# Heads of a latent attention started six turns apart instead of in pairs

## The reference

```python
def mla_attention(q, c_kv, k_rope, pos, kv_norm_w, w_uk, w_uv, q_norm_w, k_norm_w):
    ...
    ckv = rms_norm(c_kv, kv_norm_w)
    k_nope = (ckv @ w_uk).reshape(B, S, MLA_HEADS, MLA_NOPE)
    v = (ckv @ w_uv).reshape(B, S, MLA_HEADS, MLA_DV)
    k = jnp.concatenate([k_nope, jnp.broadcast_to(k_rope[:, :, None, :], (B, S, MLA_HEADS, MLA_ROPE))], axis=-1)
    q = rms_norm(q, q_norm_w)
    k = rms_norm(k, k_norm_w)
    ...
    for s0 in range(0, S, Q_BLOCK):
        s1 = s0 + Q_BLOCK
        kb, vb = k[:, :s1], v[:, :s1]
        sc = jnp.einsum('bqhd,bkhd->bhqk', q[:, s0:s1], kb, preferred_element_type=jnp.float32) * scale
        mask = chunk_id[s0:s1, None] >= chunk_id[None, :s1]
        sc = jnp.where(mask, sc, -jnp.inf)
        p = jax.nn.softmax(sc, axis=-1).astype(v.dtype)
        outs.append(jnp.einsum('bhqk,bkhd->bqhd', p, vb))
```

```python
        o_a = rms_norm(o_a, dn_norm_w[l]) * jax.nn.silu(dn_z.reshape(B, S, DN_HEADS, DN_DV))
        y_a = o_a.reshape(B, S, DN_V) @ w_out_dn[l]
        ...
        y_b = o_b.reshape(B, S, MLA_VD) @ w_out_mla[l]
        mix = jax.nn.sigmoid(gate_dn) * y_a + jax.nn.sigmoid(gate_mla) * y_b
```

## Time and profile before

| | us |
|---|---|
| median of 3 runs | 2572.59 |
| lowest and highest run | 2569.84, 2576.09 |
| profiled execution | 2570.07 |
| its span in the profile | 2568.3 |

### The profile page before, as it was taken

The page is one execution under the profiler, slowest core; times in us unless marked ns, Lnnn a source line. Parts: engine busy times, 40 slices in busy tenths (PEclk is TensorE's granted clock), DMA queues, the critical chain, the costliest instruction groups (busy, mean ns, idle before and its releaser), DMA issues.

```text
span 2568.3 us, 27012 instructions
## 1 busy us (share of the span) xinstructions
PE 2358.6 (92%) x10928; PEld 1890.4 (74%) x10928; DVE 1083.0 (42%) x1579; ACT 927.7 (36%) x1352; POOL 700.4 (27%) x417
## 2 busy tenths in 40 slices
PE   8798989997789899899999887999999999999996
PEld 4577877993467677688888676787777777888875
DVE  2476655444433432433321499513444243322333
ACT  2534424114433432533322332334552433322334
POOL 1141144001101125322223232321232353432332
PEclk9898989998899899999999898999999999999998
DMA  8222223221122123333333421232211322333341
GB/s 261 74 66 74 68 57 99 66 78 37 37 52 62 52 84 109 102 100 98 94 98 97 123 79 57 88 98 82 82 58 58 115 82 82 107 90 99 99 123 50
DMA packets 347984, 220.67 MB, mean 86 GB/s; under 512 B 18393, under 2 KB 327244, under 8 KB 347860
## 3 DMA queue, kind: packets, MB, share of 16 engines
q1 hardware_dynamic: 338462, 202.31, 27.2%
q10 hardware_dynamic: 9398, 16.62, 2.0%
HBM read 210.49 MB, written 8.41 MB: 85 GB/s over the span
## 4 chain that ended last, share of the span: by engine, by line
PE 75%; DVE 11%; ACT 8%; POOL 3%; issue 3%; DMA 1%; ACTq 0%; SPq 0%; DVEq 0%; POOLq 0%
PE ps L342 74%; DVE arena L368 4%; ACT arena L357 4%; DVE arena L360 2%; DVE scr L368 1%; PE ps L345 1%; ACT scr L357 1%; POOL wlo L360 1%; ACT whi L357 1%; ACT L353 1%; POOL arena L360 1%; DVE arena L365 1%; DVE scr L360 1%; DVE wlo L360 1%; DMA wraw<-in_w_in_dram 1%
## 5 line engine op out<-in xcount | busy, mean ns | idle before, releaser
L342 PE MATMUL ps<-hhi,whi 128*128 128x512 f32 x1664 | 679.1, 408 | 53.2 <-POOL wlo L360 30.3
L360 POOL TENSOR_TENSOR wlo<-wraw,whi 128x1024 fp32r<-128x1024 f32 (+1 forms) x164 | 391.2, 2385 | 1188.7 <-ACT whi L357 1188.7
L342 PE MATMUL ps<-hlo,whi 128*128 128x512 f32 x1664 | 662.8, 398 | 0.0
L342 PE MATMUL ps<-hhi,wlo 128*128 128x512 f32 x1664 | 661.7, 398 | 0.0
L357 ACT ACTIVATE whi<-wraw 128x1024 fp32r<-128x1024 f32 (+1 forms) x328 | 340.8, 1040 | 372.7 <-PE ps L342 304.2
L342 PEld LDWEIGHTS ps<-hhi,whi 128*128 128x128 f32 x1664 | 322.7, 194 | 133.7 <-issue 47.9
L342 PE MATMUL ps<-arena 128*128 128x128 f32 (+4 forms) x2304 | 335.4, 300 | 41.1 <-ACT arena L357 17.5
L342 PEld LDWEIGHTS ps<-hlo,whi 128*128 128x128 f32 x1664 | 322.3, 194 | 68.4 <-issue 3.7
L342 PEld LDWEIGHTS ps<-hhi,wlo 128*128 128x128 f32 x1664 | 321.1, 193 | 69.9
L360 DVE TENSOR_TENSOR wlo<-wraw,whi 128x1024 fp32r<-128x1024 f32 x164 | 213.0, 1299 | 353.0 <-ACT whi L357 352.9
L342 PEld LDWEIGHTS ps<-arena 128*128 128x128 f32 x2304 | 289.1, 197 | 72.5 <-issue 21.8
(11 more groups left out here) (190 smaller groups left out, 2678.2 us busy)
## 6 DMA issues: line engine op xcount, KB each, us to landing
wraw<-in_w_in_dram SPq DMA_DIRECT2D x99, 512.0 KB, 3.9
wraw<-in_w_ff_dram SPq DMA_DIRECT2D x64, 512.0 KB, 4.0
wraw<-in_ffn_w_up_dram SPq DMA_DIRECT2D x44, 512.0 KB, 3.9
wraw<-in_w_ada_dram SPq DMA_DIRECT2D x32, 512.0 KB, 3.9
wraw<-in_w_gate_dram SPq DMA_DIRECT2D x32, 512.0 KB, 3.9
arena<-in_w_ada_dram SPq DMA_DIRECT2D x8, 1024.0 KB, 11.7
wraw<-in_ffn_w_down_dram SPq DMA_DIRECT2D x16, 512.0 KB, 3.8
wraw<-in_w_branch_dram SPq DMA_DIRECT2D x16, 512.0 KB, 3.3
```

The lines of the kernel that those rows point to most:

```text
L342: return pe.e.matmul(o, l, r, start=start, stop=stop)
L360: return q.e.tensor_tensor(o, a, b, op)
```

## The change

Three things. `seq` and its inverse `unseq` number the query blocks head by head instead of alternating within a pair, which sets the rotation of `PTB` and what ACT's copy waits for. `mla_heads` starts a new head every six turns and gives each live head one step a turn, the older one first. The call of `weave` has 72 main turns for 38 side turns instead of 64.

```diff
         def seq(h, i):
-            return 8 * (h // 2) + 2 * i + h % 2
+            return 4 * h + i
 
         def unseq(n):
-            return 2 * (n // 8) + n % 2, n % 8 // 2
+            return n // 4, n % 4
...
             def mla_heads(self):
-                for h in range(0, 8, 2):
-                    yield from both(self.mla_head(h), self.mla_head(h + 1))
+
+                live, h, since = [], 0, 6
+                while h < 8 or live:
+                    if h < 8 and since >= 6:
+                        live.append(self.mla_head(h))
+                        h, since = h + 1, 0
+                    since += 1
+                    for g in list(live):
+                        try:
+                            next(g)
+                        except StopIteration:
+                            live.remove(g)
+                    yield
...
-            weave(f.norms_then(), side, 64, 38)
+            weave(f.norms_then(), side, 72, 38)
```

## The result

The kernel with staggered heads took 2587.46 us (median of 4 runs, 2586.50 to 2589.87) against 2571.22 of the kernel before (median of 4, 2568.99 to 2576.09): ratio 1.0071, 95% interval 1.0057 to 1.0085. So it is slower by about 0.7%, 5.5 us over the forecast of 2582 and inside its 2578 to 2590. The profiled execution took 2587.36 us, its span 2585.6.

A forecast was written before the change was run, and what follows sets the result against it. PE made 75% of the chain, so only its waits or lower clock could change. -3 + 1.7 + 9.4 + 3.1 = +11.2 on 2570.07 gave 2581.3, stated as 2582 us; range 2560 to 2597, forecast case 2578 to 2590.

The forecast's parts named there:

- C: The sixteen `gd` and `gm` steps: a lone head has links with nothing between, +9.4 us, between +1 and +13.
- S0: A head's first scores wait for the norm chain through ACT: 2.9 us each, open at heads 2 and 6.
- the bank: First transpose takes the PSUM bank the older head just left: 0.85 us at five heads, 5.9 with transpose copies.
- T3: A head's last transpose waits for DVE's normalising, now once per head: five times 0.8 us, 4.0 in all.
- Slots: Raw slots at the `uk` blocks: all ACT waits for a DMA there go; PE had lost 2.1 us at one.
- A: The norms, 606.66 to 692.45 us: `o_norms` and `z1` slip, -3 us, between -9 and +5.
- D: End of `gm` to end of `ya`: `ya` starts at 29.7 us, not 23.1; +3.1 us, between -6 and +9.
- B: End of the last `z1` step to the first `gd` step: ten turns without linear steps, +1.7 us, between -5 and +7.
- Balance: Rival over the norms to `ya`: `gd` and `gm` cost only +4, the norms give -6; about 2572 us, chance 0.22.
- faster: Rival: one head's chain fills the other's waits beside `z_gate` and `gates` too; about 2558 us, chance 0.20.
- Much slower: Rival: PE stays at 1.2 GHz over the first `gd` and `ya` steps, 12 to 15 us more; about 2595, chance 0.13.
- Doesn't do what it says: Rival: the 38/72 ratio of side steps costs, not the stagger; same sum, no chance of its own given.

The follow-up runs named there:

- e5: Staggered kernel with the younger head ahead of the older one in every turn: 2576.40 us, ratio 1.0031 to the kernel before.
- e4: Staggered kernel with 76 main turns for 38 side turns, a linear step after every second turn: 2584.41 us, ratio 1.0057 to the kernel before.
- e10: e9 with 74 main turns for 37 side turns instead of 72, a linear step exactly every second turn: 2551.33 us, ratio 0.9926 to the kernel before.
- at 74, covered: The kernel of e10: staggered heads, gate batches laid under linear steps, 74 main turns for 37 side turns: 2551.33 us.
- e11: e9 with the younger head taking its step first in each turn: 2556.10 us, ratio 0.9945 to the kernel before.
- e3: Staggered kernel with a finished head giving its PSUM output bank back one turn later: 2582.65 us, ratio 1.0054 to the kernel before.
- e9: Staggered kernel with `z_gate` and `gates` laid under linear steps, output bank returned late, 72 main turns for 37 side turns: 2568.75 us, ratio 0.9996 to before.
- the first two runs: Kernel before (pairs) with 72 main turns for 38 side turns: 2567.31 us, ratio 0.9995; staggered kernel with 64: 2587.58 us, 1.0078 to before.

## Why the prediction was right, and where it was not

**The direction and the main place: right.** C was to pay, through S0, the bank and T3, because a lone head has links with nothing between. C pays 15.1 of the 20.2. The two S0 waits (2.66, forecast 2.9), the five T0 waits (0.85, 0.69 three times, 0.84, forecast 0.85) and c0 three times (0.37) stand in the trace where they were said; the later bank took 4.8 us away. The young head first (e5), and the step behind `un` (e4, e10), each take the S0 waits of C away without taking out an instruction, so they come from the order and the phase.

**Slots: the waits went, as said.** ACT waited for `in_w_in` seven times before, 15.9 us, and once 3.83 us for the first block of `ya`; after it has no wait for a DMA from 600 us to `yb`. The price was wrong: beside the 2.2 of A, I named 2.1 us of PE. The trace of before has 2.13 at 751.54 and also 5.97 at 875.01, which is the 3.83 of ACT and a DVE add of 2.45 behind it. I had left that one in D's loss without its name, so D hides 4.5 us won (1.43 is left of it, at 891.82) under 9.5 lost.

**A: mis-sized.** -0.5 for -3. The terms that I named add up to -4.3 (-4, +3.6, -2.2, -1.7), and I took -3 without saying for what. The waits for ACT in the norms went from 11.8 to 5.1 us, 6.7 won for the 4 said, and the DMA wait is gone. But two more rotations stand open and not one, 6.2 lost for 3.6. And the sum had no term for head 0's S0, which now lies in A:

```profile
683.80 0.99 PE L342 MATMUL ps<-arena 128*128 128x128 f32 x4 [2.32 <-DVE arena L368]
```

Behind it the last `z1` step ran with matmuls of 0.63 us and took 7.1 us instead of 5.4, so the 1.7 that the DMA wait had cost came back.

**B: near.** +0.6 for +1.7: 33.4 us for a walk of 32.8 and 1.7 for the clock.

**C: mis-sized, +15.1 for +9.4, by three terms left out of the sum.** First the slow matmuls behind each open S0, 1.0 and 1.6 us; I had added such a term in B and D, where the gaps were over 4 us, and left it out in C. Second DVE's add beside POOL's split, which stood as the end of the range (+13) and is the rule: `un` waits 0.46 in three heads, 1.4 in all. In the kernel after, POOL and DVE at 764:

```profile
764.08 2.35 POOL L360 TENSOR_TENSOR wlo<-wraw,whi 128x1024 fp32r<-128x1024 f32 x1 [33.85 <-ACT whi L357]
...
765.02 1.96 DVE L360 TENSOR_TENSOR scr<-scr,arena 128x512 f32<-128x512 f32 x1 [1.87 <-ACT scr L357]
```

and at 74, covered, where no split of POOL runs beside it:

```profile
731.34 0.68 DVE L360 TENSOR_TENSOR scr<-scr,arena 128x512 f32<-128x512 f32 x1
```

Third, and the largest, what a break costs beyond its listed wait: the sum took the waits alone for the loss. The listed waits and slow matmuls of C come to 16.1 us of its loss of 21.4, so this is 5.3 us. In the three middle heads it is 1.0 each, as worked out from start to start above; in the others it was not taken apart. Against these, three terms came out smaller than said: T3 (0.71 twice and 0.16 three times for 0.8 five times) by 2.1 us, T0 with c0 (4.9 for 5.9) by 1.0 and S0 by 0.5. The waits that the sum priced thus come to 12.1 us for 15.7: it was near only because it gave those too much and the rest nothing.

**D: near.** +5.0 for +3.1; `ya` started 31.0 us behind `gm` (said 29.7), and T1 waited behind `split_o`'s lows, as said. PE, then DVE:

```profile
915.04 0.69 PE L345 MATMUL ps<-cst,scr 128*128 128x128 f32 x2 [4.10 <-DVE scr L364]
915.38 0.78 PE L342 MATMUL ps<-hhi,whi 128*128 128x512 f32 x1
```

```profile
909.02 4.69 DVE L360 TENSOR_TENSOR hlo<-arena,hhi 128x512 fp32r<-128x512 f32 x3 [0.34 <-ACT hhi L357]
```

**Behind `ya`: not foreseen.** "Everything keeps its order" was true, but 2.9 us came back. The first 73 matmuls of `yb` took 18.2 us before at a granted clock of 0.91 and 16.6 after at 1.00, 1.6 of the 2.9; the rest lies spread behind. Before, then after:

```profile
950.39:968.61 18.22, 18.22 (x73) 14.92 (x74) 7.22 (x6) 10.99 (x18) 9.74 (x6) 0.91 0.51 163
```

```profile
970.61:987.22 16.61, 16.61 (x73) 13.76 (x74) 7.18 (x6) 10.98 (x18) 9.77 (x6) 1.00 0.56 173
```

The span grew by 17.3 where the sum said 11.2. The 6.1 between are +5.7 in C, +2.5 in A and +1.9 in D, less 1.1 in B and 2.9 behind `ya`: the forecast came as near as it did because the last two took part of C's error back, and that is luck: a change of 17.3 was forecast as 11.2.

**The rivals.** *Balance* and *faster* fell in C. (The sum of *faster* took 4 us off D; its own 25 us for `ya` gives a loss of 25 - 12.7 + 2.8 + 1.5 = 16.6, 1.6 less than before, so it should have said 2560.) The *faster* one was half right in what it named: e10, like e11 clearly faster than both kernels, shows that one head's chain can fill the other's waits, and saves 17.0 us at `yb` against before, where the rival said 12. But it has the linear steps at other turns, the later bank and the covered batches together. The even phase alone (e4) and the later bank alone (e3) stayed slower than before, and e9 shows that bank and cover do not do it without the phase; how much e10 needs of each was not taken apart. That its place was ACT's queue in B was wrong: B is +0.6 in the kernel after. *Much slower* (the clock over the first steps of `gd` and `ya`) came true only in the first step of `ya`, 2.8 us, which the sum held and which before had too (8.3 us for that step, after 8.2). *Doesn't do what it says* (the ratio) is refuted by the first two runs.

## What to carry over

Here versions with the stagger came out between 0.8% slower and 0.7% faster than the kernel before, and two of them (e9, e10) differ in nothing but where the linear steps fall. So the order alone does not decide: price each link by whether a long piece of other work is queued between producer and consumer, turn by turn, and fix the phase (an integer number of fillers per chain, placed behind the links that cost most) before judging the order. Write beside each open wait also what the engine runs slower behind it, and take the price of a break from start to start, not from the listed wait. And ask of every buffer that is handed round which turn gives it back: a bank given back in the same turn in which the next head takes one is a wait built into the order.

## What the runs showed of the hardware that I had not expected

- A DVE add of two SBUF operands (128x512) took 0.68 us alone, and 1.96 or 2.45 when POOL's split of 2.35 had started before it; each ended 0.55 us after the split did. The Trainium skill (GPSIMD Engine Reference, Specifications) names contention with DVE instructions of two SBUF inputs; the trace agrees, 1.3 to 1.8 us for one add. It went by who started first: in the kernel after, an add at 727.29, 0.34 us ahead of a split, took 0.69 us, and that split 2.59.
- A wait of PE of 2.66 us was followed by five matmuls of up to 0.73 us instead of 0.40 (738.16 to 740.29), while after the waits of 0.69 and 0.37 at 785 the linear step began with 0.45 and went on with 0.39. The granted clock of the whole of C was 0.98, against 1.00 before. The price is not fixed: in e9 the steps behind four S0 waits of 2.66 took 7.2, 7.9, 8.0 and 5.5 us, and in the kernel before the step behind a wait of 2.13 (751.54) took 5.9, as much as a step behind `uk` with no wait. What decides it is open.
- The same work, `yb`, behind the same 2.31 us wait for `ob`, ran at a granted clock of 0.91 in one kernel and 1.00 in the other. What decided it is open.
